# Half of the down projections' tile pairs as seven block products (Strassen), with their weight sums split by ScalarE and GpSimd

## What is computed

```python
def conv_ffn(x, w_up, w_conv, b_conv, w_down):
    h = causal_dwconv(x @ w_up, w_conv, b_conv)
    gate, val = jnp.split(h, 2, axis=-1)
    return (jax.nn.silu(gate) * val) @ w_down

# second_block, per layer
h = h + mix
h = h + conv_ffn(rmsnorm(h, ffn_norm_g[layer]), ffn_w_up[layer], ffn_conv_w[layer],
                 ffn_conv_b[layer], ffn_w_down[layer])
```

## Time and profile before

| | |
|---|---|
| median of 3 runs | 1990.55 us (1989.06 to 1993.39) |
| the profiled execution | 1985.93 us, its span 1984.2 us |
| mean granted TensorE clock | 0.986 of 2.4 GHz |
| first up tile of layer 0 | starts at 1061.7 us |
| DMA | 168.72 MB, mean 85 GB/s |

### The profile page before, as it was taken

How to read it: one execution, slowest core, us unless ns; L and a number is a source line. 1 busy time by engine, 2 the same in 40 slices (tenths; PEclk the granted TensorE clock), 3 DMA queues, 4 the chain that set the end, 5 groups by cost and what they waited for, 6 DMA issues and landing times.

```text
span 1984.2 us, 29514 instructions
## 1 busy us (share of the span) xinstructions
PE 1893.5 (95%) x11647; PEld 1564.6 (79%) x11647; DVE 1064.2 (54%) x1511; ACT 895.2 (45%) x1239; POOL 725.6 (37%) x527
## 2 busy tenths in 40 slices
PE   5999999998989999989899999999999999999997
PEld 4887888886877888768657888888888788888886
DVE  5123777775267656868985551354434555513543
ACT  4344777776246445462334442344333344423432
POOL 1323222224211112143514454454545544544543
PEclk8999999999999999999999999999999999999999
DMA  8221113114111111131212333232333223232331
GB/s 308 67 69 40 65 55 107 55 54 160 54 51 61 47 55 54 54 107 65 74 34 94 97 95 96 96 96 96 95 96 96 95 81 101 95 97 96 96 96 54
DMA packets 48825, 168.72 MB, mean 85 GB/s; under 512 B 5552, under 2 KB 7856, under 8 KB 48688
## 3 DMA queue, kind: packets, MB, share of 16 engines
q1 hardware_dynamic: 46384, 162.03, 25.1%
q10 hardware_dynamic: 2304, 4.81, 0.7%
HBM read 164.72 MB, written 2.10 MB: 84 GB/s over the span
## 4 chain that ended last, share of the span: by engine, by line
PE 83%; DVE 10%; ACT 4%; issue 1%; DMA 1%; POOL 0%; ACTq 0%; SPq 0%; DVEq 0%
PE ps L576 25%; PE ps L577 24%; PE ps L578 24%; PE ps L707 3%; PE ps L726 2%; ACT sq L1113 2%; DVE X L1644 1%; DMA raw<-in_units 1%; PE ps L610 1%; DVE wS L2166 1%; DVE wS L1638 1%; DVE hf L1818 1%; PE ps L893 1%; DVE hf L1638 1%; DVE sp L1638 1%
## 5 line engine op out<-in xcount | busy, mean ns | idle before, releaser
L1621 POOL TENSOR_TENSOR wlo<-raw,whi 128x512 fp32r<-128x512 f32 x482 | 651.7, 1380 | 1022.9 <-ACT whi L1095 1022.9
L1095 ACT ACTIVATE whi<-raw 128x1024 fp32r<-128x1024 f32 x251 | 258.5, 1056 | 500.7 <-PE ps L578 486.4
L576 PE MATMUL ps<-Ahi,whi 128*128 128x512 f32 (+1 forms) x784 | 308.3, 393 | 13.7 <-POOL wlo L1621 6.4
L577 PE MATMUL ps<-Alo,whi 128*128 128x512 f32 (+1 forms) x784 | 304.8, 389 | 0.0
L578 PE MATMUL ps<-Ahi,wlo 128*128 128x512 f32 (+1 forms) x784 | 303.3, 387 | 0.0
L576 PEld LDWEIGHTS ps<-Ahi,whi 128*128 128x128 f32 x784 | 148.1, 189 | 49.6 <-issue 8.5
L1638 DVE TENSOR_TENSOR ps<-ps,rstd 128x1024 f32<-128x1024 f32 (+1 forms) x60 | 69.7, 1162 | 208.3 <-PE ps L578 176.0
L578 PEld LDWEIGHTS ps<-Ahi,wlo 128*128 128x128 f32 x784 | 148.2, 189 | 31.1
L577 PEld LDWEIGHTS ps<-Alo,whi 128*128 128x128 f32 x784 | 148.3, 189 | 29.9 <-issue 0.5
L1644 DVE SCALAR_TENSOR_TENSOR cv<-ps,vec,cv 128x511 f32<-128x511 f32 (+1 forms) x176 | 131.9, 749 | 70.6 <-ACT cv L1113 66.0
L576 PE MATMUL ps<-Fhi,whi 128*128 128x512 f32 (+1 forms) x427 | 166.0, 389 | 3.4 <-DVE Flo L1638 3.4
(11 more groups left out here) (296 smaller groups left out, 3858.1 us busy)
## 6 DMA issues: line engine op xcount, KB each, us to landing
raw<-in_units SPq DMA_DIRECT2D x299, 512.0 KB, 3.5
X<-in_xT SPq DMA_DIRECT2D x4, 512.0 KB, 9.4
X<-in_xT ACTq DMA_DIRECT2D x4, 512.0 KB, 5.2
out_xT<-X SPq DMA_DIRECT2D x8, 256.0 KB, 2.3
CX<-in_ctxT SPq DMA_DIRECT2D x4, 256.0 KB, 9.7
acc<-in_rope ACTq DMA_DIRECT2D x1, 384.0 KB, 3.2
gmw<-in_gmw ACTq DMA_DIRECT2D x1, 384.0 KB, 4.2
bs<-in_bs ACTq DMA_DIRECT2D x1, 384.0 KB, 4.7
```

The costliest lines, as they stand in the source:

```text
L576: nc.tensor.matmul(out, sh, mh, start=first, stop=False)
L577: nc.tensor.matmul(out, sh, ml, start=False, stop=False)
L1095: nc.scalar.activation(whi[:, s % CONV, :], raw[:, c % RAW, :], ACT.Copy).then_inc(sem("whi"), 1)
L1621: lo = nc.gpsimd.tensor_tensor(wlo[:, s % CONV, cols], raw[:, plan.unit_at[("split", s)] % RAW, cols], whi[:, s % CONV, cols].bitcast(fp32 ...
```

## The change

The parts become 12 and 10 rows (`FR`). Of a part's four pairs of down tiles (m = 2p, 2p+1), two are computed by Winograd's form of Strassen's scheme: pairs 1 and 3 in part 0, pairs 1 and 2 in part 1 (`SEVENS`). For each pair and each two K rows (a quad) the 2 x 2 weight blocks and the 2 x 2 activation blocks (two K rows by two halves of 256 tokens) give seven block products of 256 columns in place of eight. It needs:

- four sums of activations per two rows (T1 to T4), made by VectorE (`forms`) from the float32 rows, split by ScalarE (`forms_high`) and GpSimd;
- four sums of weight blocks per quad, made by VectorE from `raw` (`summed`). Two quads are a unit: a split "sums" of six blocks (three sums of each quad) and a split "blocks" of eight (three plain blocks and the fourth sum of each). Both are copied by ScalarE and lowered by GpSimd, 768 and 1024 columns;
- seven results per pair gathered by VectorE in nine operations (`seven_results`).

On ScalarE `convert` stops at such splits; `convert_to(end)` copies them, and ordinary ones up to `end`, waiting on a new count `used` that TensorE gives when it is done with a split, or on the PSUM count where there is none. In part 1 of layer 0 `feed` runs `convert_to` up to the last unit, then its loop over m; VectorE runs `downs(..., 3)`, the results of pairs 0 to 2, ahead of its loop.

```diff
+SEVENS = {(0, 0): [1, 3], (0, 1): [1, 2], (1, 0): [1, 3], (1, 1): [1, 2]}
...
+        def seven(l, f, pairs):
+            quads = [(p, q) for p in pairs for q in range(FR[f] // 2)]
...
+            units = [quads[i:i + 2] for i in range(0, len(quads), 2)]
...
+                for i in mine:
+                    for s in (at + 2 * i, at + 2 * i + 1):
+                        self.last["split", s] = len(self.free) - 1
...
+            def seven(l, f, i):
+                s_sums, s_blocks, quads = plan.sevens[i]
+                end = FR[f] // 2 - 1
+                for n, (s, forms) in enumerate(((s_sums, 3), (s_blocks, 4))):
+                    lows(s)
+                    for x in range(forms):
+                        for o, (p, q) in enumerate(quads):
...
+                            if n == 0:
+                                at, mov, opens = [(yb[:, T:T + HT], form(T3), True), (ya[:, T + HT:2 * T], form(T1), True),
+                                                  (yb[:, 0:HT], form(T2), True)][x]
+                            else:
+                                at, mov, opens = [(yb[:, HT:T], block(0, 0), False), (ya[:, T:T + HT], form(T4), False),
+                                                  (ya[:, HT:T], block(1, 1), True), (ya[:, 0:HT], block(1, 0), False)][x]
...
+                            if n == 1 and x == 3 and q == end:
+                                last.then_inc(sem("psum"), 2)
...
+                    if s in plan.used:
+                        last.then_inc(sem("used"), 1)
...
-                    if s >= CONV and plan.last[("split", s - CONV)] > n:
+                    if s in plan.part or s >= CONV and plan.last[("split", s - CONV)] > n:
                         break
...
+            def convert_to(end):
+                while converted[0] <= end:
+                    s = converted[0]
+                    was = plan.freed_by[s]
+                    if was in plan.used:
+                        ac.wait_ge(sem("used"), plan.used[was])
+                    else:
+                        ac.wait_ge(sem("psum"), plan.last[("split", was)] + 1)
...
+                if end[0] == "dn":
+                    convert_to(plan.sevens[plan.groups[end[1:]][-1]][1])
                 for m in range(8):
                     psum(("evb", m // 2) if end[0] == "ev" and m < 4 else (*end, m))
...
                     if f == 0:
-                        for m in range(8):
-                            psum(("dn", l, f, m))
+                        psum(("dn", l, f, 0))
+                    forms_high(l, f, FR[f] // 2 - 1)
+                    if f == 0:
+                        convert_to(plan.dn_end[l, f])
...
+            def summed(i):
...
+                tt(two(to[:, 0:4 * P]), w21, two(u[:, 0:4 * P]), ADD, "s13")
+                tt(to[:, 4 * P:6 * P], to[:, 0:2 * P], u[:, 2 * P:4 * P], ADD, "s2")
+                tt(u[:, 4 * P:6 * P], to[:, 4 * P:6 * P], u[:, 6 * P:8 * P], ADD, "s4")
+            def seven_results(l, f, p):
+                m = 2 * p
+                ya, yb = psum(("dn", l, f, m)), psum(("dn", l, f, m + 1))
+                ts(held, yb[:, HT:T], 1.0, None, MUL)
+                tt(vsum, yb[:, 0:HT], held, SUB)
+                tt(qsum, yb[:, T:T + HT], vsum, ADD)
+                tt(wsum, ya[:, T + HT:2 * T], vsum, ADD)
+                tt(X[:, m, :], ya[:, 0:T], X[:, m, :], ADD)
+                tt(X[:, m, 0:HT], X[:, m, 0:HT], held, ADD)
+                tt(X[:, m, HT:T], X[:, m, HT:T], wsum, SUB, "resid")
+                tt(X[:, m + 1, :], ya[:, T:2 * T], X[:, m + 1, :], ADD)
...
+                tt(row, row, qsum.rearrange("p (o t) -> p o t", o=1).to_broadcast([P, 2, HT]), ADD, "resid")
...
+            def forms(l, f, q, odd):
...
+                tt(t_raw[:, T1, :], a2, a1, SUB)
+                ve.wait_ge(sem("hi"), made[0])
+                tt(t_raw[:, T3, :], a2, b2, SUB)
+                tt(t_raw[:, T2, :], b2, t_raw[:, T1, :], SUB)
+                tt(t_raw[:, T4, :], b1, t_raw[:, T2, :], SUB, "tr")
```

More of the change, by code:

```diff
@@ L22 @@
 DFF = 2816
-FH = DFF // P // 2
+FR = [12, 10]
+F0 = [0, 12]
+FT = DFF // P
+assert sum(FR) == FT
 EPS = 1e-6
@@ L309, in ffn @@
                     if f == j == 0:
                         norm(f"ffn{l}")
-                w = lambda m, ks: [(f"dn{l}", f * FH + k, m) for k in ks]
-                tile(("dn", l, f, 0), [("resid", RAT[f"f{l}{f}"] + 2)], w(0, range(FH - 1)))
+                end = FR[f] - 1
+                w = lambda m, ks: [(f"dn{l}", F0[f] + k, m) for k in ks]
+                before = len(self.free)
+                tile(("dn", l, f, 0), [("resid", RAT[f"f{l}{f}"] + 2)], w(0, range(end)))
                 tile(("dn", l, f, 1), [("resid", RAT[f"f{l}{f}"] + 2)],
-                     w(1, range(FH - 1)) + w(0, [FH - 1]) + w(1, [FH - 1]), beside=("dn", l, f, 0))
@@ L315, in ffn @@
-                for m in range(2, 8):
-                    tile(("dn", l, f, m), [("resid", RAT[f"f{l}{f}"] + m + 1)], w(m, range(FH)))
+                     w(1, range(end)) + w(0, [end]) + w(1, [end]), beside=("dn", l, f, 0))
+                self.leaves(before)
+                pairs = SEVENS[l, f]
+                for p in range(1, 4):
+                    if p in pairs:
+                        if p - 1 not in pairs:
+                            seven(l, f, [x for x in range(p, 4) if all(y in pairs for y in range(p, x + 1))])
+                        continue
+                    before = len(self.free)
+                    for m in (2 * p, 2 * p + 1):
+                        tile(("dn", l, f, m), [("resid", RAT[f"f{l}{f}"] + m + 1)], w(m, range(FR[f])))
+                    self.leaves(before)
@@ L351, in __init__, with leaves @@
                 self.first_use.setdefault(i // UT, n)
+    def leaves(self, before):
+        for n in range(before, len(self.free)):
+            for i in range(self.first[n], self.first[n] + self.count[n] - 1):
+                if i % UT == UT - 1:
+                    self.used[i // UT] = len(self.used) + 1
 PLAN = Plan()
@@ L468, in build @@
         Ehi, Elo = place(25088, "Ehi", [KD, T], fp22), place(29184, "Elo", [KD, T], fp22)
-        Bhi, Blo = place(14336, "Bhi", [KD, T], fp22), place(18432, "Blo", [KD, T], fp22)
+        Bhi, Blo = place(15360, "Bhi", [KD, T], fp22), place(19456, "Blo", [KD, T], fp22)
+        Thalf = [place(23552 + 512 * i, f"T{i}", [2, HT], fp22)[:, :, :] for i in range(23)]
         step = tmp[:, 0, :]
@@ L1011, in ffn @@
+            ended = []
             def ffn(l):
                 for f in range(2):
-                    for j in range(FH):
+                    for j in range(FR[f]):
                         tile(("up", l, f, j))
                         for part in range(2):
-                            last = linear(("up", l, f, j), *((Ahi, Alo) if l else (Bhi, Blo)), 0, SAT[f"ffn{l}"] + 1, XO, offset=KD * part,
+                            last = linear(("up", l, f, j), Bhi, Blo, 0, SAT[f"ffn{l}"] + 1, XO, offset=KD * part,
@@ L1036, in _ @@
                 for part in range(2):
-                    last = linear(("ch", m), Ahi, Alo, 0, SAT["mix1"] + 1, XO, offset=KD * part,
+                    last = linear(("ch", m), Bhi, Blo, 0, SAT["mix1"] + 1, XO, offset=KD * part,
                                   ks=list(range(KD)), col0=T * part)
@@ L2232, in ahead @@
                         tt(acc[:, 0:T], first, sq[:, g % 3, 0:T], ADD, "n_acc")
+                if end[0] == "dn":
+                    downs(*end[1:], 3)
                 for m in range(8):
@@ L2236, in feed @@
                         resid(("evb", m // 2), m, at=m % 2 * T)
-                    elif end[0] == "dn" and m < 2:
-                        resid((*end, 1), m, at=m * T)
-                    else:
+                    elif end[0] != "dn" or m >= 6:
                         resid((*end, m), m)
@@ L2306, in _ @@
             flush()
-            feed("ffn1", "ffn_g1", ("od",), Ahi, Alo)
+            feed("ffn1", "ffn_g1", ("od",), Bhi, Blo)
             ffn(1)
+            downs(1, 1, 3)
             for m in range(7):
-                resid(("dn", 1, 1, max(m, 1)), m, at=T if m == 1 else 0)
+                if m == 6:
+                    resid(("dn", 1, 1, 6), 6)
                 if m:
@@ L2383, in _arrays @@
                 units[c, :, j, :] = w["ada_w"][layer][j * P:(j + 1) * P, chunk * P:(chunk + 1) * P]
-            elif i * UT + j < len(PLAN.split):
+            elif i * UT + j < len(PLAN.split) and PLAN.split[i * UT + j] is not None:
                 name, k, m = PLAN.split[i * UT + j]
```

257 lines of the change are left out of this document (198 added, 59 removed).

## The result

| | before | changed |
|---|---|---|
| median of the session's runs | 1989.8 us | 2048.85 us (2047.35 to 2051.67) |
| profiled execution, its span | 1985.93, 1984.2 us | 2051.67, 2049.9 us |
| mean granted clock | 0.986 | 0.978 |

The changed kernel takes 1.0297 times as long (95% interval 1.0277 to 1.0316), 59 us more. The forecast was 2021 with a range up to 2036: the side was right, the size was half of what came.

What follows compares the result with a forecast made beforehand. TensorE's issue rate was taken as the bound from 1150 us on. Terms -12.1 + 3.6 + 8.1 + 13.3 + 11.0 + 6.8 = +30.7 took the profiled 1985.93 to 2016.6; median forecast 2021 us, range 2006 to 2036.

Steps and rivals of the forecast that it cites:

- Padding of splits costs DMA only: In the weight splits: filling them up with blanks adds DMA and no other time; no term in the sum.
- The gain: On TensorE in the block-product down tiles: 0.28 us saved per quad, 44 quads, -12.1 us.
- The first split behind the last unit: TensorE waits for late copies: 4.05 us at part 0 to 1, twice; before part 1's tile 6, 13.3 and 11.0.
- rival 1: At the four long stops: splits found ready, by earlier copies or a finer count, saving kept, 1982 us; chance 0.05.
- The first sums: At the start of part 1's downs: GpSimd's first sums 1.3 us late, blocks 0.5 more; twice 1.8, +3.6 us.
- The clock: Behind the four long stops: the granted clock falls, 1.7 us lost at each, +6.8; bounds nothing or twice that.
- Rival 2: In the units: GpSimd becomes the bound, 6.0 us a unit against 4.94, 23 us more, 2044 us; chance 0.10.
- 4.9 us per unit against 4.94: In the steady units: GpSimd's time beside VectorE's additions against TensorE's, almost no slack, 0 us taken.
- Nobody else is crowded: Beyond GpSimd in the units: VectorE's and ScalarE's added operations fit beside an 11 us up tile and stay hidden.
- The lock rule: On the port pair shared by VectorE and GpSimd: exclusive lock, the loser blocks for the whole instruction; would give Rival 2.
- Rival 3: At block-product matmuls: weight loads overlap nothing, 9 x 0.189 us per quad, 75 us more, 2096 us; chance 0.02.
- Rival 4: In the whole change: it makes no block products, contrary to its description; no chance of its own.

Runs made afterwards that it cites:

- run 1: Changed kernel with each part's blocks filled up with blanks to a whole split, in the plan only: 2024.24 us, ratio 1.0181 to the kernel before.
- run 2: Kernel before, no block products, with four blank blocks ahead of layer 1's mixer and four ahead of its part 0 downs: 2017.55 us, ratio 1.0144.
- run 3: Changed kernel with convert_to going two splits further at the end of part 0: 2034.42 us, ratio 1.0229 to the kernel before.
- run 4: Changed kernel with convert_to running to the end of part 1's downs, so tile 6's copies precede the squares: 2029.09 us, ratio 1.0200.
- run 5: Changed kernel with the edits of run 1, run 3 and run 4 together: 1989.62 us, ratio 1.0006 to the kernel before.
- run 6: Changed kernel with the edits of run 1 and run 3, part 1's norm begun earlier and T's last low parts after the first unit's: 1992.68 us.
- run 7: Kernel of run 6 with three pairs by block products in part 0 of each layer: 2000.97 us, ratio 1.0056 to the kernel before.
- run 8: Changed kernel with only a part's last T low parts made by GpSimd after the first unit's: 2054.24 us, ratio 1.0319 to the kernel before.

## Why the prediction was wrong, point by point

- **The failed step: "Padding of splits costs DMA only"**, with "Rows are only regrouped (12 and 10 for 11 and 11), the other products stay". The products stayed, their place in the splits did not. The end of a part moved to the middle of a split, and 24.6 us of stops came in stages that the diff doesn't touch (runs 1 and 2). With it the sum would have been +55, 2046 us on the scale of the forecast, for 2048.85 measured: it is most of the 28 us by which the forecast missed. I had read that a slot is freed by a finished tile, and used this only for the splits next to the block products; the count of blocks from one tile boundary to the next split boundary, in every stage behind the change, was what I left out.
- **"The gain"**: 0.275 us a quad, -12.1. Right in size, partly by luck. Without the stops of over 0.3 us the 22 units took 109.7 us, for 108.8 by the forecast's 0.1177. But that is 1.8 us gained by matmuls at 0.1133 and 2.7 lost in small stops. "256 columns cost more than half of 512" compared the slower pace at 256 columns with the faster one at 512; pace by pace it is 0.1133 to 0.2289 and 0.1177 to 0.2334, and the saving of a quad between two matmul rows of the faster pace is 0.37 us.
- **"The first split behind the last unit"**: 4.05 twice, measured 4.03 twice; 13.3, measured 14.25; 11.0, measured 11.18. All by the mechanism given; runs 3 and 4 remove them by the two ways that rival 1 named. Of the 13.3, most of what was missing is in the last step: GpSimd's low part, taken at its lone 2.54 us, took 3.4 beside VectorE's additions for the next rows.
- **"The first sums"**: mechanism right, size low: +3.6, measured 5.3. I missed that T's low parts stand ahead of the sums on GpSimd and so stretch VectorE's additions (1.40 us for 256 columns, taken 0.83), and, in part 0 of layer 1, the shift by four blocks, which goes with it in run 1.
- **"The clock"**: +6.8, measured 10. A term mis-sized: the low stretches here lasted 4 to 7 us, for the row's 3.4. My own upper bound, 13.6, held it. The same four stops cost 7.4 in run 1, so one trace gives this term to some 3 us only.
- **Rival 1** (no stops): refuted in each of the four places, and made true by hand in run 5. Most of the difference from its 1982 is what the long stops had covered: VectorE's tail at the part's end.
- **Rival 2** (GpSimd the bound): its mechanism is there, at a fifth of its size. GpSimd's 6.0 us a unit doesn't exist; it is 5.15, over TensorE's 4.95, and in the units of part 1 TensorE starts its blocks when GpSimd is done. That costs 0.2 us a unit, not 1.06, and some 2 us in all. In part 0, with three units in a row, it shows once or not at all. So "4.9 us per unit against 4.94" was 0.25 too low, and "I take 0 for the steady units" a term too small. "Nobody else is crowded" failed too: it left out that VectorE's additions, 1.55 us alone, take 5.03 of a unit's 5.15 beside GpSimd. Runs 6 to 8 show that each delay of either comes out at TensorE.
- **The lock rule** (the Trainium skill, SBUF — State Buffer, "Who interferes with whom"): the page calls the shared ports an exclusive lock. Blocking for a whole instruction it states of VectorE's two-port modes; of additions with both inputs in SBUF, as these are, it says that they contend with GpSimd's reads. If the lock kept the two engines' instructions wholly apart, a unit would take the sum of their lone times, 4.45 + 1.55 = 6.0 us. In run 5 both are done in 5.15, so the times overlap in part. GpSimd's 512 columns take 1.59 us for 1.27 and VectorE's 256 columns 1.40 for 0.43; by the unit GpSimd loses 0.7 us and VectorE 3.5. Interference there is, borne mostly by VectorE.
- **Rival 3** (loads show): 14.86 us for the 126 matmuls and 126 loads of three units, where the loads alone, at 0.189 us each, would be 23.8; refuted.
- **Rival 4**: the block products are there.

## What to carry to other kernels

Where buffers are freed at the grain of a finished piece of work, the alignment between pieces and buffers is part of the schedule: after any change of counts or padding, print for each later stage how much of the first buffer is left at a tile's start and hold it against the refill time. When stops are removed, ask what they covered: here two engines with no slack (GpSimd 5.15 us a unit against 4.95, VectorE in the units and in the norm) stood behind stops of 11 to 14 us, and a gain, 9 us, only came out where the new work was taken away from the part that has a norm behind it. A list of waits can hide a bound: hold the period of a repeated stage against each engine's own time in it, since many small stops stand in no list of the long ones. A scheme that saves a tenth of the products is worth using exactly where its helpers have room.
